# Finishing the convolution branch and starting the first head pair beside the last projections, with the last two modulation chunks through one weight buffer

## The reference

```
mod = silu(c) @ ada_w + ada_b                    # 6 x 1024 values for each of two conditionings
h   = rmsnorm(x) * (1 + sc1) + sh1
p   = h @ w_in                                   # 1024 x 2944: groups A (1920), B (512), C (512)
A:  p = p + mu * (centred_shift(p) - p); r, k, v, decay, rates from it
    two scans (forward, backward) over tokens for 8 heads of 64, from a given state
    y = headnorm(sum of both) + bonus, gated
B:  gelu, layernorm, 128x128 spatial mixing, product, rmsnorm
C:  glu, depthwise convolution of width 31, layernorm, silu, rmsnorm
x   = x + gt1 * (concat(A, B, C) @ w_out)
x   = x + gt2 * moe(adaLN(rmsnorm(x)))           # 16 experts, 2 used per token
y   = rmsnorm(x)
```

## Time and profile before

| | |
|---|---|
| median of 3 runs | 1019.83 us (1019.49 to 1020.84) |
| profiled execution, its own time | 1026.58 us |
| its span, first to last instruction | 1024.8 us |
| PE busy | 804.2 us (78%) |
| DVE busy | 483.7 us (47%) |
| ACT busy | 286.0 us (28%) |
| POOL busy | 127.1 us (12%) |
| mean granted PE clock | 0.865 |

### The profile page before, as it was taken

One profiled execution on the slowest core, in us unless ns is written; L12 is line 12 of the kernel. 1 busy time (PEld: TensorE's weight loads), 2 busy tenths in 40 slices (PEclk: granted clock), 3 DMA queues, 4 the chain that ended last, 5 costly groups with the idle time before them and its releaser, 6 DMA issues. The chain is left out here.

```text
span 1024.8 us, 18048 instructions
## 1 busy us (share of the span) xinstructions
PE 804.2 (78%) x7510; PEld 500.6 (49%) x7510; DVE 483.7 (47%) x1024; ACT 286.0 (28%) x589; POOL 127.1 (12%) x129
## 2 busy tenths in 40 slices
PE   3489999999933829979699956999279999999700
PEld 3345455655522527767578742455244544444300
DVE  1210047665355996889989750524601111111145
ACT  2222014122145444646543610101011111111143
POOL 3000000000004030210300000000022222221041
PEclk9589999999965755969889977999579999999955
DMA  7952044054080000000000048101189999999362
GB/s 278 340 197 82 0 165 164 31 217 165 1 277 3 1 1 2 7 24 2 8 3 8 4 154 332 61 25 46 26 306 382 358 349 357 367 344 370 109 227 82
DMA packets 42442, 150.58 MB, mean 147 GB/s; under 512 B 6031, under 2 KB 8598, under 8 KB 37398
## 3 DMA queue, kind: packets, MB, share of 16 engines
q1 hardware_dynamic: 33142, 78.07, 21.2%
q0 software_dynamic: 9216, 71.31, 18.7%
HBM read 133.08 MB, written 22.05 MB: 151 GB/s over the span
## 5 line engine op out<-in xcount | busy, mean ns | idle before, releaser
L2178 PE MATMUL banks<-arena 128*128 128x512 f32 x304 | 156.9, 598 | 0.0
L1724 PE MATMUL banks<-arena 128*128 128x512 f32 x288 | 128.4, 599 | 1.1 <-ACT arena L1344 1.1
L2177 PEld LDWEIGHTS banks<-arena 128*128 128x128 f32 x304 | 57.6, 192 | 73.0 <-issue 71.2
L1724 PEld LDWEIGHTS banks<-arena 128*128 128x128 f32 x288 | 55.2, 192 | 70.7 <-issue 69.0
L1748 PE MATMUL banks<-arena 128*128 128x512 f32 x144 | 65.1, 595 | 1.4 <-DVEq L1158 1.0
L1590 DVE TENSOR_TENSOR arena<-arena,banks 128x256 f32<-128x256 f32 x18 | 7.6, 421 | 122.2 <-ACT arena L1350 115.6
L2177 PE MATMUL banks<-arena 128*128 128x128 f32 x304 | 59.8, 279 | 1.5 <-ACT arena L201 1.5
L2057 DVE TENSOR_TENSOR arena<-arena 128x641 f32<-128x641 f32 x15 | 12.4, 828 | 99.6 <-ACT arena L1922 99.6
L775 DVE TENSOR_TENSOR arena<-arena 128x30 f32<-128x30 f32 (+14 forms) x120 | 52.3, 436 | 4.1
L2047 DVE SCALAR_TENSOR_TENSOR arena<-arena 128x640 f32<-128x640 f32 x60 | 49.8, 879 | 0.0
L772 DVE TENSOR_TENSOR arena<-arena 128x30 f32<-128x30 f32 (+14 forms) x120 | 45.7, 381 | 2.7
(11 more groups left out here) (347 smaller groups left out, 1515.3 us busy)
## 6 DMA issues: line engine op xcount, KB each, us to landing
arena<-in_ada_w_dram SPq DMA_DIRECT2D x12, 2048.0 KB, 12.7
arena<-in_w_in_dram SPq DMA_DIRECT2D x5, 2048.0 KB, 14.5
slot_rows<-arena SPq DMA_DIRECT2D x18, 512.0 KB
arena<-modulations SPq DMA_DIRECT2D x8, 512.0 KB, 7.4
h_rows<-arena SPq DMA_DIRECT2D x5, 512.0 KB, 2.6
out_dram<-arena SPq DMA_DIRECT2D x5, 512.0 KB, 2.6
arena<-in_x_sample_dram SPq DMA_DIRECT2D x4, 512.0 KB, 10.8
arena<-in_w_out_dram SPq DMA_DIRECT2D x1, 2048.0 KB, 10.7
```

What stands on the lines that cost most here:

```text
L1724: x = T_.matmul(ps[2 + s][:, :], hT[:, s, c, :], wgu[:, s, c, :], start=(c == 0), stop=(c == KD - 1))
L2177: T_.matmul(ctx_[:, 0:P], w, h1T[:, k, 0:P], start=(k == 0), stop=(k == KD - 1))
L2178: x = T_.matmul(lat[:, :], w, h1T[:, k, P:T], start=(k == 0), stop=(k == KD - 1))
```

## The change

- The convolution's taps on DVE: 4 before and 7 after the mixing of each tile n (before: 2 and 3), so that they end at n = 5.
- The convolution's tail moves between the tiles: transposes behind PE's tile 7, statistics at DVE's n = 7, norm at n = 8, silu and squares at ACT's n = 9, scale at DVE's n = 10, transposes back behind tile 11, copies at ACT's n = 12. Branch B's transposes back move from behind tile 10 to behind tile 9.
- Thirteen steps of pair 0 (`EARLY`) leave the scan: PE puts its six parts (`low_rank` four times, `key_norm` twice) between the k steps of tiles 13 and 14, all through one double bank, each waiting until ACT or DVE has read the one before; ACT does its part before copying tiles 13 and 14, DVE after mixing tiles 12 and 13.
- The first 8192 columns of the arena (ring buffers 0 and 1) now hold those early tiles, so loads 16 and 17 (ada 10, ada 11) both go through buffer 2: load 16 waits for the matmul of ada 9, load 17 for that of ada 10.
- `scan_act`, `scan_pool`, `scan_dve` and `scan_pe` walk the rest; two of the three bank memsets go. `scan_loads` is untouched.
- `PLAN` is a new order of the same steps.

```diff
@@
+        def slot(n):
+            return n % 4 if n < 16 else 2
+        def before(n):
+            return n - 4 if n < 16 else 2 * n - 18
         def wslot(n):
-            return (wring01 if n % 4 < 2 else wring23)[:, n % 2, :, :]
+            return (wring01 if slot(n) < 2 else wring23)[:, slot(n) % 2, :, :]
...
-            low_rank 0 0 0 / low_rank 0 1 0 / decay 0 0 / low_rank 0 0 1 / decay 0 1 / key_square 0 0 / low_rank 0 1 1 / key_square 0 1 /
-            key_norm 0 0 / key_norm 0 1 / mix 0 / kk 0 0 / factors 0 0 / factors 0 1 / init 0 / kk 0 1 / operands 0 0 / operands 0 1 /
-            gram 0 1 / gram 0 0 / diag 0 / bonus 0 / low_rank 1 0 0 / sub 0 1 / low_rank 1 1 0 / sub 0 2-3 / low_rank 1 0 1 / sub 0 4-6 /
...
+            low_rank 0 0 0 / low_rank 0 1 0 / low_rank 0 0 1 / key_square 0 0 / low_rank 0 1 1 / key_square 0 1 / decay 0 0 / decay 0 1 /
+            key_norm 0 0 / key_norm 0 1 / mix 0 / kk 0 0 / kk 0 1 / factors 0 0 / init 0 / operands 0 0 / factors 0 1 / operands 0 1 /
+            gram 0 1 / gram 0 0 / diag 0 / bonus 0 / low_rank 1 0 0 / low_rank 1 1 0 / sub 0 1-8 / low_rank 1 0 1 / key_square 1 0 /
...
+        EARLY_PE = {(2, 2, 3): EARLY[0], (2, 2, 4): EARLY[1], (2, 2, 5): EARLY[2], (2, 2, 6): EARLY[4], (2, 3, 2): EARLY[8], (2, 3, 4): EARLY[9]}
...
+        def early_temp_free(pe, key):
+            i = EARLY_AT[key]
+            if i:
+                pe.wait_ge(*at("read_" + EARLY_TEMPS[i - 1][0], EARLY_TEMPS[i - 1]))
+            else:
+                pe.wait_ge(*at("catBC"))
...
         def scan_pool(pool):
             g = nc.gpsimd
+            pool.wait_ge(*at("mixed", 3))
+            pool_steps(pool, EARLY)
+            pool.wait_ge(*at("mixed"))
...
             g.memset(wb[:, :, :, :, :], 0.0).then_inc(*up("wb_zero"))
...
         def scan_dve(dve):
-            v = nc.vector
-            dve.wait_ge(*at("yc_T", NT - 1))
-            dve.wait_ge(*at("catBC"))
+            dve.wait_ge(*at("late_mod_row", 11))
+            nc.vector.memset(ps[0][:, :], 0.0).then_inc(*up("temp_zero"))
...
             def ring_load(n):
                 kind, j = RING[n]
                 if n >= 4:
-                    sp.wait_ge(*last_use(n - 4))
+                    sp.wait_ge(*last_use(before(n)))
...
+                if (c, m) == (2, 2):
+                    act_steps(act, EARLY[0:8])
+                if (c, m) == (2, 3):
+                    act_steps(act, EARLY[8:])
...
-                for _ in range(2):
+                for _ in range(4):
...
-                for _ in range(3):
+                for _ in range(7):
...
+                        if (c, m, k) in EARLY_PE:
+                            pe_steps(pe, [EARLY_PE[c, m, k]])
...
+                    if a_i == 7:
+                        pe.wait_ge(*at("conv_tap", 2 * CONV_K - 1))
+                        pe.wait_ge(*at("gmlp_prod", NT - 1))
...
+                if n == 12:
+                    dve_steps(dve, EARLY[0:8])
+                if n == 13:
+                    dve_steps(dve, EARLY[8:])
```

More of the change, by code:

```diff
@@ L310, in build @@
         pos[0] = VT1
-        EARLY_END = VT1
+        qt = carve(2 * 2 * 64).rearrange("p (i h n) -> p i h n", i=2, h=2)
+        stio = carve(2 * P).rearrange("p (d c) -> p d c", d=2)
+        stin, stout = stio[0:64], stio[64:128]
+        assert pos[0] == 2 * KD * 512
+        qr0 = carve(2 * 2 * TS).rearrange("p (d i t) -> p d i t", d=2, i=2)
+        bks = [x.rearrange("p (d s i t) -> p d s i t", d=2, s=NCH, i=2)
+               for x in (carve(2 * 2 * TS), catBC[:, :, :].rearrange("p c t -> p (c t)"))]
         inva = carve(1024).rearrange("p (h s q) -> p h s q", h=2, s=16)
@@ L343, in build @@
[L343 to L354, removed]
@@ L359, in build @@
[L359 to L366, removed]
@@ new lines, in build @@
+            keys 0 1 / sub 0 9-10 / low_rank 1 1 1 / sub 0 11 / decay 1 0 / xloc 0 1 / decay 1 1 / sub 0 12-19 / key_square 1 1 /
+            sub 0 20 / key_norm 1 0 / sub 0 21-22 / key_norm 1 1 / sub 0 23-24 / keys 0 0 / sub 0 25 / mix 1 / sub 0 26-27 / xloc 0 0 /
+            factors 1 0 / sub 0 28-30 / turn 0 / factors 1 1 / kk 1 0 / off 0 / kk 1 1 / operands 1 0 / merge_a 0 / merge_b 0 /
+            operands 1 1 / gram 0 2 / gram 0 3 / diag 1 / wqx 0 1 / sub 1 1-2 / keys 0 2 / mr 0 1 / wqx 0 0 / sub 1 3 / keys 0 3 /
@@ new lines, in build @@
+            bonus 1 / sub 1 4-9 / low_rank 2 0 0 / sub 1 10 / mr 0 0 / low_rank 2 1 0 / chain 0 2 / sub 1 11 / decay 2 0 / low_rank 2 0 1 /
+            xloc 0 2 / chain 0 0 / gram 0 4 / sub 1 12 / decay 2 1 / sub 1 13-14 / chain 0 3 / wqx 0 2 / chain 0 1 / xloc 0 3 / mr 0 2 /
+            keys 0 4 / sub 1 15 / key_square 2 0 / sub 1 16-17 / low_rank 2 1 1 / sub 1 18 / chain 0 4 / sub 1 19 / wqx 0 3 / sub 1 20 /
+            key_square 2 1 / sub 1 21 / xloc 0 4 / key_norm 2 0 / sub 1 22 / mr 0 3 / chain 0 5 / state_out 0 / sub 1 23-25 / wqx 0 4 /
@@ new lines, in build @@
+            chain 0 6 / sub 1 26 / key_norm 2 1 / sub 1 27-28 / mr 0 4 / sub 1 29 / mix 2 / sub 1 30 / y 0 0 / chain 0 7 / factors 2 0 /
+            turn 1 / kk 2 0 / y 0 2 / off 1 / factors 2 1 / chain 0 8 / kk 2 1 / y 0 3 / merge_a 1 / operands 2 0 / y 0 1 / merge_b 1 /
+            y 0 4 / operands 2 1 / head_stats 0 / gram 1 1 / gram 1 0 / diag 2 / keys 1 1 / keys 1 0 / xloc 1 1 / bonus 2 / sub 2 1-3 /
+            low_rank 3 0 0 / sub 2 4-6 / wqx 1 1 / xloc 1 0 / sub 2 7-10 / gram 1 2 / sub 2 11 / keys 1 2 / mr 1 1 / sub 2 12 / wqx 1 0 /
@@ new lines, in build @@
+            gram 1 3 / xloc 1 2 / gram 1 4 / sub 2 13 / init 1 / sub 2 14 / keys 1 3 / mr 1 0 / sub 2 15 / wqx 1 2 / chain 1 2 / keys 1 4 /
+            head_centre 0 / sub 2 16 / mr 1 2 / sub 2 17-18 / low_rank 3 1 0 / chain 1 0 / sub 2 19-20 / low_rank 3 0 1 / chain 1 3 /
+            xloc 1 3 / xloc 1 4 / sub 2 21 / decay 3 0 / chain 1 1 / wqx 1 3 / chain 1 4 / key_square 3 0 / sub 2 22 / low_rank 3 1 1 /
+            mr 1 3 / decay 3 1 / key_square 3 1 / state_out 1 / chain 1 5 / sub 2 23-24 / wqx 1 4 / key_norm 3 0 / key_norm 3 1 / mr 1 4 /
@@ new lines, in build @@
+            chain 1 6 / sub 2 25 / mix 3 / y 1 0 / sub 2 26 / chain 1 7 / kk 3 0 / y 1 2 / sub 2 27 / factors 3 0 / chain 1 8 / y 1 3 /
+            sub 2 28-29 / y 1 1 / sub 2 30 / head_scale 0 / y 1 4 / factors 3 1 / turn 2 / gram 2 1 / kk 3 1 / off 2 / keys 2 1 /
+            gram 2 0 / merge_a 2 / keys 2 0 / head_gain 0 / merge_b 2 / operands 3 0 / operands 3 1 / xloc 2 1 / gram 2 2 / head_bias 0 /
+            xloc 2 0 / head_bonus 0 / head_stats 1 / init 2 / diag 3 / sub 3 1 / wqx 2 1 / keys 2 2 / sub 3 2 / mr 2 1 / gram 2 3 /
@@ new lines, in build @@
+            head_centre 1 / sub 3 28-29 / gram 3 1 / sub 3 30 / gram 3 0 / turn 3 / keys 3 1 / keys 3 0 / xloc 3 1 / head_scale 1 / off 3 /
+            gram 3 2 / xloc 3 0 / merge_a 3 / gram 3 3 / head_gain 1 / merge_b 3 / init 3 / head_bias 1 / head_bonus 1 / wqx 3 1 /
+            keys 3 2 / mr 3 1 / wqx 3 0 / xloc 3 2 / keys 3 3 / head_stats 2 / mr 3 0 / wqx 3 2 / chain 3 2 / chain 3 0 / xloc 3 3 /
+            gram 3 4 / head_centre 2 / keys 3 4 / head_scale 2 / mr 3 2 / chain 3 3 / chain 3 1 / head_gain 2 / wqx 3 3 / head_bias 2 /
@@ L542, in scan_pool, with pool_steps @@
             g.memset(ec[:, :, :], 1.0).then_inc(*up("end_one"))
-            for st in SCHEDULE:
+            pool_steps(pool, REST)
+            post_pool(pool)
+        def pool_steps(pool, steps):
+            g = nc.gpsimd
+            for st in steps:
                 k = st[0]
@@ L562, in scan_pool, with act_steps @@
                     g.tensor_tensor(ktb[:, 0, :], ktb[:, 0, :], ktb[:, 1, :], ALU.add).then_inc(*up("kt_sum", m))
-            post_pool(pool)
         def scan_act(act):
-            a = nc.scalar
             act.wait_ge(*at("mod_stored0", 10))
             act.wait_ge(*at("mod_stored1", 11))
-            for st in SCHEDULE:
+            act.wait_ge(*at("mixed"))
+            act_steps(act, REST)
+            post_act(act)
+        def act_steps(act, steps):
+            a = nc.scalar
+            for st in steps:
                 k = st[0]
@@ L695, in scan_act, with dve_steps @@
                         .then_inc(*up("act_did", ("head_rstd", m)))
-            post_act(act)
         def scan_dve(dve):
-            v = nc.vector
-            dve.wait_ge(*at("yc_T", NT - 1))
-            dve.wait_ge(*at("catBC"))
+            dve.wait_ge(*at("late_mod_row", 11))
+            nc.vector.memset(ps[0][:, :], 0.0).then_inc(*up("temp_zero"))
             dve.wait_ge(*at("mod_stored0", 10))
             dve.wait_ge(*at("mod_stored1", 11))
[L704 to L707, removed]
+            dve_steps(dve, REST)
+            post_dve(dve)
+        def dve_steps(dve, steps):
+            v = nc.vector
+            for st in steps:
                 k = st[0]
@@ L824, in scan_dve, with pe_steps @@
                         .then_inc(*up("state_next", (m, s)))
-            post_dve(dve)
         def scan_pe(pe):
```

(34 more changed lines are left out.)

112 lines of the change are left out of this document (60 added, 52 removed).

## The result

The changed kernel takes 1030.89 us (median of 4 runs, 1027.31 to 1032.49) against 1019.66 us (4 runs), outside the range given (1011 to 1027). The medians lie 11.2 us apart. Run once more beside the experiments the changed kernel gave 1.010 (1.007 to 1.0129).

A forecast was written before the change was run, and what follows sets the result against it. PE bounds the projections, then a gap, then mostly DVE; the work taken out of the gap returns as a wait for the state load. First gram +0.5 us, new order 0, so 1020.3 us, range 1011 to 1027.

The forecast's parts named there:

- row 10 at 276: Near the projections' end, ACT's copy of the row of ada 10, held by row 8's store, ends near 276.
- the wait at the spatial matmuls: PE waits there for branch B's norm, delayed by added DVE taps: 0 to 3.2 us, taken as 1.3.
- PE's standstill: In tile 13, PE stops before low_rank 0 1 0 because ACT has not read the double bank: 4.1 us.
- The delay of row 11: ACT's copy of ada 11's row moves by 1.3 + 2.6 + 7.6 + 4.1 = 15.6 us, to 299.5.
- One small term: Between early steps in the last tiles, a PE k step of 1.09 us was said to cover each ACT read.
- The queue: In SP's queue, small transfers do not pass large ones: row 8's store and the state load wait behind bulk transfers.
- the store passes: Rival: row 8's 1 KB store passes the 2 MB load, no wait in tile 13; 1016.2 us, chance 0.10.
- the state load doesn't bind: Rival: at the scan's start the state lands at once, first gram 17.2 us earlier; 1002.6 us, chance 0.06.
- The clock falls in the wait: Rival: PE's clock falls in tile 13's wait, up to +7 us; 1022.8 to 1027.3 us, chance 0.20.
- the likeliest case: As worked out, without a clock fall in tile 13: 1020.3 us, own range 1017.5 to 1023, chance 0.42.
- I price it at 0: New order of scan steps from 331 on: 0, ±4 us usual, ±10 far bound; chances 0.12 faster, 0.10 slower.
- +0.5 forecast: First gram at the scan's start comes at 331.5 against 331.07, held by the late state load: +0.5 us.

The follow-up runs named there:

- e5: Changed kernel with twelve idle matmuls (3.8 us) put in front of the second early low_rank, where PE stood still; ratio 0.9993 to the kernel before.
- e1: Changed kernel with the stores of modulation row 8 issued ahead of the load of ada 11; ratio 0.9996 to the kernel before.
- e2: Changed kernel with pair 0's two 32 KB state loads issued ahead of the three fills and the branch store; ratio 0.9982 to the kernel before.
- e4: Kernel before with only the new PLAN, the written-out order of the scan steps; ratio 1.003 to the kernel before.
- e8: Kernel before with only pair 0's state loads issued ahead of the fills; ratio 0.9988 to the kernel before.
- e10: Kernel before with only loads 16 and 17 (ada 10, ada 11) put through buffer 2; ratio 0.9992 to the kernel before.
- e11: Changed kernel run again, unaltered, beside other experiments; ratio 1.01 (1.007 to 1.0129) to the kernel before.
- e3: Changed kernel with both row 8's stores ahead of ada 11's load and pair 0's state loads ahead of the fills; ratio 0.9886 to the kernel before.
- e9: Changed kernel with row 8's stores and pair 0's state loads issued first, old scan order, POOL's two memsets exchanged; 1004.68 us, ratio 0.985 to the kernel before.
- e6: Changed kernel with the scan steps behind pair 0's early ones in the kernel before's order; ratio 1.0049 to the kernel before.
- the first four experiments: e1, e2, e3 and e4, each timed beside the kernel before; ratios 0.9996, 0.9982, 0.9886 and 1.003.

## Why the prediction was wrong

**The early part held.** Forecast and measured: row 10 at 276 and 276.1; its wait released by the store, yes; the wait at the spatial matmuls 1.3 and 1.1 us; PE's standstill 4.1 and 3.8 us; the operands 5.1 and 5.1 us. The delay of row 11 by turns, early steps and waits was given as 15.6 us, to 299.5 with the copy's end; e5, in which the clock does not fall, has it at 299.2. One small term was put at nothing: a k step of 1.09 us does not cover the first of ACT's reads, which begins with a table load of 1.28 us, and 0.97 us of standstill stays in e1 without the store's wait.

**The queue held.** The small transfers did not pass the large ones: ACT waited 7.65 us for a 1 KB store behind one weight load, and the 32 KB state loads landed 20.5 us after their issue, behind the fills and the store of `catBC`:

```profile
arena<-in_state_rwkv_dram SPq DMA_DIRECT2D x2, 32.0 KB, 20.5
```

PE waited 25.35 us for them, part of it before they were issued. From the issue of the fills (308.50) to PE's transposes (332.33) are 23.8 us; the prediction had 24.8. The Trainium skill's rule (DMA: Bandwidth & Descriptors, section on queues, rings and completion order) that descriptors are taken in ring order agrees with both, and with e1 and e2, where issuing first was enough. The rival "the store passes" and the rival "the state load doesn't bind" fell.

**The step that failed is "The clock falls in the wait".** The prediction read from the gap at 284.8 that the clock falls some 5 us into a standstill, held 4.1 us to be short of it, and took the clock's holding as the likeliest case. It fell 2.7 us after PE's last matmul. One gap in one execution had given one number, and that was the longest of all: the same gap, behind the same projections, was profiled again in e4, where the clock fell 2.3 us after the last matmul (283.73 + 1.31 = 285.04; the mean of 0.84 in 286 to 288 puts the fall near 287.4).

```profile
283.73 1.31 PE L2203 MATMUL banks<-ident,arena 128*128 128x128 f32 x10
```

```profile
286.00:288.00 2.00, 0.00 (x0) 0.00 (x0) 1.63 (x10) 0.87 (x2) 0.00 (x0) 0.84 1.53 524
```

In e8 and e10 it was 2.7 and 2.0 us. So the 5 us were no bound from below, and the case that rested on them should have had the lower chance. The size of the rival was nearly right: up to 7 us for three k steps and three early steps, while PE ran at half clock for 16 us, which takes 8 us more than at full clock; e5 against the changed kernel has 7.6 us at row 11. But each rival was priced alone. The clock's fall by itself ended at 1027.3; the measured time holds it together with the next miss.

**The second miss is the term "I price it at 0".** The new order costs 0.003, 3 us, by the timed runs of e4 (1.0011 to 1.0049). With the 7.25 us by which the first gram is later this makes 10.3, against the measured 9.7 and, in e11, 10. So the parts are: +0.5 forecast, about +7 from the clock at the gram, +3 from the order. The sum closes, but within intervals of several us, and the share of the order is the soft one. Whether and why the new order is slower is not shown by any trace. Six profiled executions with the old order have 264.2 to 272.8 us from gram to reload, seven with the new 266.7 to 273.9; from the gram to the end of the span it is 684.2 to 693.7 and 686.0 to 694.3, with means of 689.0 and 688.8. The spread within one order is larger than the 3 us, so these profiles cannot place it.

**What the change was good for.** The work it moves is really out of the gap; two waits in SP's queue, and the clock that fell in the first of them, took the gain. With both removed the same change is 12 us faster than the kernel before (e3, ratio 0.9886), and 15 us with the old order and the memsets exchanged (e9, 0.985). One edit alone (e1 or e2) only brings it back to even.

## What to carry to other kernels

When work is moved ahead, ask what the first consumer after the gap waits for besides that work, above all a small transfer that was hidden by the old slack and is queued behind bulk transfers nobody is waiting for; issue it first. When a buffer is shared to make room, list what stands behind the later load in the issuing queue and which engine waits for that, since the same wait was free in e10 and cost 10 us in the changed kernel. A short standstill of PE in a dense stretch can cost more afterwards than while it lasts: the one of 3.8 us here cost 7.6 us more through the clock, and filling it with useless matmuls gave back 10 us of the time.

## What the runs showed of the hardware that was not expected

How long PE stood still before the granted clock fell to 0.50 differs from execution to execution, at one place of one program. In the gap behind the projections it was 5.1 us in the kernel before, 2.3 in e4, 2.7 in e8 and 2.0 in e10, whose matmuls around the gap are the same. In the standstill of tile 13 it was 2.7 us in the changed kernel, 2.0 in e11, 2.3 in e2 and 3.6 in e6. (The times are from PE's last matmul, whose end is modelled, to the fall as the mean clock of short stretches gives it.) Every profiled standstill of 3.4 to 3.8 us lost the clock; the one of 1.0 us in e1 kept it.

Once fallen, the clock stayed at 0.50 for 16 us of a fully busy PE (278.5 to 294.5). In all four executions with this standstill (the changed kernel, e2, e6, e11) it came back only 3 to 5 us after the last early `low_rank` of tile 13. In e1 and e5 the same mix of steps ran with the clock at 1.00 and did not lower it. The runs don't show whether the kind of matmul matters for the return.

Executions of one kernel differ by more than expected: 25 of the kernel before beside the first four experiments lie between 1016.14 and 1028.82 us. From the first gram to the reload the same instructions took 272.8 us in the profiled execution of the kernel before, and 268.8 in e10, which has the same instructions there. A single profiled execution therefore does not measure differences of a few us in the scan, while row 10 is copied within 1.1 us at the same time in executions of kernels that agree up to there, apart from e6, where it came 4 us later.
